# Moving a decay chain under a linear layer, and a compression under memory attention, in a two-block transformer kernel

## What is computed

```python
# gated linear attention (GLA) layer; memory of 256 tokens, 4 heads of 128
q, k, v, r, alr, mq = split_cols(h @ w_in, [256, 256, 512, 512, 16, 512])
log_a = log_sigmoid(alr @ w_alpha + b_alpha) / 16
o = gla_chunked(q, k, v, log_a)          # cumulative decays scale q and k; state scan over chunks
o = rmsnorm(o, g_head) * silu(r)
m = mem_attend(mq, mem_k, mem_v)         # softmax(mq mem_k^T) mem_v
x = x + concat([o, m]) @ w_out

# sparse attention (NSA) layer
k_c, v_c, k_s, v_s, k_w, v_w = split6(rmsnorm(x) @ w_kv)
k_cmp = gelu(blocks(k_c + pe_k) @ w_ck1) @ w_ck2      # 31 compressed blocks; the same for v
p_cmp = masked_softmax(q k_cmp^T + bias) * gate       # "compressed weights"
o = p_cmp v_cmp + gate * attention(q, k_s, v_s) + gate * attention(q, k_w, v_w)
m = mem_attend(mq, mem_k, mem_v)
x = x + concat([o, m]) @ w_out
```

## Time and profile before

| | us |
|---|---|
| median of 3 runs | 3510.04 (3506.98 to 3519.47) |
| the profiled execution | 3506.27 (its span 3504.5) |
| PE busy in it | 3334.3 (95%) |
| DVE busy | 1746.9 (50%) |
| ACT busy | 1274.3 (36%) |
| POOL busy | 334.0 (10%) |

### The profile page before, as it was taken

The page is one execution under the profiler, slowest core; times in us unless marked ns, Lnnn a source line. Parts: engine busy times, 40 slices in busy tenths (PEclk is TensorE's granted clock), DMA queues, the critical chain, the costliest instruction groups (busy, mean ns, idle before and its releaser), DMA issues. The chain is left out here.

```text
span 3504.5 us, 52430 instructions
## 1 busy us (share of the span) xinstructions
PE 3334.3 (95%) x21106; PEld 2738.0 (78%) x21106; DVE 1746.9 (50%) x2634; ACT 1274.3 (36%) x1870; POOL 334.0 (10%) x277
## 2 busy tenths in 40 slices
PE   7999999799999999999899999978999997899998
PEld 5888879588888888879778888866888875578886
DVE  4444364554443444365454443446665355666642
ACT  3222355632222222355642222334222232542222
POOL 0000315300000000133500000010000001400000
PEclk9999999899999999999999999999999998999999
DMA  3332320023332333320023333302333250023332
GB/s 115 96 100 99 107 72 4 29 90 97 97 103 90 98 96 103 112 78 15 15 79 96 97 103 102 126 29 74 99 97 104 95 176 10 13 79 97 98 102 81
DMA packets 73605, 295.72 MB, mean 84 GB/s; under 512 B 8160, under 2 KB 9056, under 8 KB 72288
## 3 DMA queue, kind: packets, MB, share of 16 engines
q1 hardware_dynamic: 73440, 293.32, 25.9%
HBM read 291.19 MB, written 2.10 MB: 84 GB/s over the span
## 5 line engine op out<-in xcount | busy, mean ns | idle before, releaser
L438 PE MATMUL bank<-src_hi,tile_hi 128*128 128x512 f32 x2736 | 1078.6, 394 | 26.2 <-DVE tile_lo L514 25.3
L440 PE MATMUL bank<-src_hi,tile_lo 128*128 128x512 f32 x2736 | 1065.5, 389 | 0.0
L439 PE MATMUL bank<-src_lo,tile_hi 128*128 128x512 f32 x2736 | 1065.1, 389 | 0.0
L514 DVE TENSOR_TENSOR tile_lo<-raw_tiles,tile_hi 128x1024 fp32r<-128x1024 f32 (+1 forms) x486 | 625.2, 1312 | 76.1 <-ACT tile_hi L465 59.4
L438 PEld LDWEIGHTS bank<-src_hi,tile_hi 128*128 128x128 f32 x2736 | 514.1, 188 | 145.3 <-DVE tile_lo L514 25.7
L439 PEld LDWEIGHTS bank<-src_lo,tile_hi 128*128 128x128 f32 x2736 | 514.3, 188 | 112.3 <-issue 6.7
L440 PEld LDWEIGHTS bank<-src_hi,tile_lo 128*128 128x128 f32 x2736 | 514.0, 188 | 107.4
L465 ACT ACTIVATE tile_hi<-raw_tiles 128x1024 fp32r<-128x1024 f32 (+1 forms) x486 | 526.9, 1112 | 103.4 <-DMA raw_tiles<-in_b_in 33.1
L438 PE MATMUL bank<-hid_hi,tile_hi 128*128 128x512 f32 x1312 | 514.3, 392 | 25.2 <-DVE tile_lo L514 25.2
L439 PE MATMUL bank<-hid_lo,tile_hi 128*128 128x512 f32 x1312 | 513.4, 391 | 0.0
L440 PE MATMUL bank<-hid_hi,tile_lo 128*128 128x512 f32 x1312 | 513.3, 391 | 0.0
(11 more groups left out here) (329 smaller groups left out, 3177.6 us busy)
## 6 DMA issues: line engine op xcount, KB each, us to landing
raw_tiles<-in_gu SPq DMA_DIRECT2D x264, 512.0 KB, 3.5
raw_tiles<-in_down SPq DMA_DIRECT2D x96, 704.0 KB, 4.0
raw_tiles<-in_w_in SPq DMA_DIRECT2D x46, 512.0 KB, 3.5
raw_tiles<-in_a_in SPq DMA_DIRECT2D x17, 512.0 KB, 3.6
raw_tiles<-in_w_out SPq DMA_DIRECT2D x16, 512.0 KB, 3.6
raw_tiles<-in_w_mem SPq DMA_DIRECT2D x16, 512.0 KB, 3.5
masks<-in_masks SPq DMA_DIRECT2D x4, 1948.0 KB, 8.6
raw_tiles<-in_b_in SPq DMA_DIRECT2D x9, 512.0 KB, 3.5
```

Source lines behind the costliest of these rows:

```text
L438: nc.tensor.matmul(bank, wh, hi[:, kk, 0:p.n], start=(kk == 0), stop=False)
L439: nc.tensor.matmul(bank, wh, lo[:, kk, 0:p.n], start=False, stop=False)
L440: mm = nc.tensor.matmul(bank, wl, hi[:, kk, 0:p.n], start=False, stop=last and (p.kind == "gated" or s == p.h - 1))
L514: v.tensor_tensor(self.tile_lo[:, t, 0:kc * P], self.tile_raw[:, t, 0:kc * P], self.tile_hi[:, t, 0:kc * P].bitcast(F32), ALU.subtract).th ...
```

## The change

1. **Decay chain under `a_in`.** The 17 tiles are taken in a new order: `alr` first, then q, k, r, v, mq. The decay chain (and the four SiLU) leaves the GLA phase and hangs on the tiles of `a_in`, in the steps given by `DECAYED_AT = (7, 12)`, its temporaries now in `mix`. PE's code for `a_in` is no longer a loop but written out.
2. **GLA steps closer.** The scaled k is turned in step 0, v in step 1, key-value products in steps 3 and 6 (before 9 and 11), scans in 3, 4, 6, 7 (before 9 to 12), scores in 9, outputs in 12 and 13, squares in 14 and 15. The prefetch of the output weights no longer waits for the decays.
3. **NSA.** Gates, compression and compressed weights are no phases of their own: they are hung on the steps of the memory attention, which moves ahead of `attention_pairs`. The prefetch for the output product is issued in `attention_pairs`.
4. 56 semaphores for each of two alternating phases instead of 48.

```diff
+A_IN_ORDER = [16, *range(0, 4), *range(8, 12), *range(4, 8), *range(12, 16)]
+DECAYED_AT = (7, 12)
@@ chain, tensor
-                    if p.heads:
+                    if p.heads or p.decays:
                         for i in range(1, p.m):
                             tile(i, i, 0)
+                                self.decay_products(pe, own, p, i)
@@ chain, scalar and vector: at the end of body(i)
+                        if p.decays:
+                            self.decay_activations(act, own, p, i)
+                            self.decay_vectors(dve, own, p, i)
@@
+    def decay_products(self, pe, own, p, i):
+        if i == DECAYED_AT[0] - 1:
+            pe.wait_ge(own["beside_loaded"], p.beside_landed)
+            pe.wait_ge(own["bank_free"], p.tiles + 1)
+            for cc in range(2):
+                self.nc.tensor.matmul(self.banks[2 + cc][:, :], w[0:16, cc * P:(cc + 1) * P], self.pj(16)[0:16, :], ...)
+    def decay_activations(self, act, own, p, i):
+        for cc, first in enumerate(DECAYED_AT):
+            if i == first + 1:
+                act.wait_ge(own["magnitude"], cc + 1)
+                nc.scalar.activation(mag, mag, ACT.Exp, scale=-1.0)
+                nc.scalar.activation(mag, mag, ACT.Ln, bias=self.c("one"))
+            if i == first + 3:
+                act.wait_ge(own["summed_up"], cc + 1)
+                nc.scalar.activation(ein, cum, ACT.Exp, scale=1.0 / 16)
+                nc.scalar.activation(eout, cum, ACT.Exp, scale=-1.0 / 16)
+        if i == DECAYED_AT[1] + 2:
+            for h in range(4):
+                nc.scalar.activation(self.pj(8 + h), self.pj(8 + h), ACT.Silu)
+    def decay_vectors(self, dve, own, p, i):
+            if i == first:        # bias, absolute value, minimum: 3 operations
+            if i == first + 2:    # waits logged_z; subtraction, scan
+            if i == first + 4:    # waits decays_ready; k*eout, q*ein, ends, kt
@@ gla_products
+        if s == 0:    # turn the scaled k: 8 transposes
+        if s == 1:    # waits kt_copied_a, kt_copied_v, values_copied; turn v: 16 transposes
-        if s in (9, 11):
+        if s in (3, 6):   # key-value products; s == 6 waits scanned 16
-        if s == 7:
+        if s == 9:        # scores; waits scanned 30
-        if s in (13, 14):
+        if s in (12, 13): # outputs; waits masked
@@ memory_attention(nsa=True)
+    def nsa_sums(self, pe, own, s):
+        if s == 0:        # 4 transposes of the gates
+        if 2 <= s <= 5:   # compression: 8 of 32 matmuls in each step, waits arranged
+        if s in (7, 9):   # waits gelu_ready; 2 transposes
+        if s == 10:       # waits gelu_copied; 8 matmuls
+        if s == 12:       # waits kept; 16 score matmuls with the compressed keys
+        if s in (16, 17): # waits weights_ready; 8 transposes each
+    def nsa_activations(self, act, own, s):
+        # s == 0: Sigmoid; s in (4, 6): Tanh; s in (13, 14): Exp; s in (16, 18): two copies each
+    def nsa_vectors(self, dve, own, s):
+        # s < 4: two arrange operations each; (4, 6): five GELU operations; (5, 7): the sixth; (7, 9): a copy
+        # 8: eight bias operations; 10: four copies; (12, 13): add, max, floor, subtract; (14, 15): sum, reciprocal, gates, multiply
@@ nsa_layer
-        self.nsa_gates(gates_flat)
-        self.compress(...)
-        self.compressed_weights(k_cmp, gates, turned)
-        self.attention_pairs(pairs, HD ** -0.5, values=[(kv[:, 3, :], vs), (kv[:, 5, :], vw)])
-        self.memory_attention(4, [self.mix[:, 4 + c, :] for c in range(4)], ahead=("b_out", 0, KD, 2))
+        self.memory_attention(4, [self.mix[:, 4 + c, :] for c in range(4)], nsa=True)
+        self.attention_pairs(pairs, HD ** -0.5, values=[(kv[:, 3, :], vs), (kv[:, 5, :], vw)], ahead=("b_out", 0, KD, 2))
```

More of the change, by code:

```diff
@@ L1623, in gla_weights @@
         return self.pj(17)[:, 0:2 * P]
[L1625 to L1631, removed]
+    GLA_SIGNALS = ("v_turned", "v_copied_a", "v_copied_v", "scores", "masked", "kt_turned", "kt_copied_a", "kt_copied_v", "kv_product", "scanned",
+                   "product", "stored", "squared", "summed", "logged", "rstd_ready", "normed")
@@ L1654, in gla_products @@
         if s == 0:
[L1655 to L1665, removed]
-                    mm = nc.tensor.transpose(tile(banks[6 + h % 2], i), tile(self.pj(4 + h), i), self.c("ident", P))
-                mm.then_inc(own["v_turned"], 1)
@@ L1668, in gla_products @@
-        if s == 7:
-            pe.wait_ge(own["scaled"], 2)
-            pe.wait_ge(own["v_copied_a"], 2)
-            pe.wait_ge(own["v_copied_v"], 2)
             for cc in range(2):
                 for i in range(NT):
-                    for e in range(2):
-                        mm = nc.tensor.matmul(tile(banks[4 + 2 * cc + e], i), tile(self.pj(2 + cc)[rows[e], :], i), tile(self.pj(cc)[rows[e], :], i),
-                                              start=True, stop=True)
-                mm.then_inc(own["scores"], 1)
@@ L1698, in gla_products @@
             mm.then_inc(own["kv_product"], 1)
-        if s in (13, 14):
-            cc = s - 13
-            if cc == 0:
-                pe.wait_ge(own["scanned"], 2 * (NGC - 1))
+        if s == 9:
+            pe.wait_ge(own["scanned"], 2 * (NGC - 1))
+            for cc in range(2):
+                for i in range(NT):
+                    for e in range(2):
+                        mm = nc.tensor.matmul(tile(banks[4 + 2 * cc + e], i), tile(self.pj(2 + cc)[rows[e], :], i), tile(self.pj(cc)[rows[e], :], i),
+                                              start=True, stop=True)
+                mm.then_inc(own["scores"], 1)
+        if s in (12, 13):
+            cc = s - 12
+            pe.wait_ge(own["masked"], 2 * cc + 2)
             for e in range(2):
@@ L1805, in gla_vectors @@
+        if s in (3, 4, 6, 7):
+            first = 4 * (s - 3 - s // 5)
+            for c in range(first, min(first + 4, NGC - 1)):
                 dve.wait_ge(own["kv_product"], 1 + c // 8)
@@ new lines, in weights_memory, with nsa_cleared @@
+    def weights_memory(self):
+        both = [self.units("arena", at, 2).rearrange("p u t -> p (u t)").rearrange("p (c i e w) -> p c i e w", c=4, i=NT, e=2) for at in (28, 30)]
+        return both + [self.small[:, i * 32:i * 32 + 32].rearrange("p (c i e) -> p c i e", c=4, i=NT) for i in range(3)]
+    def nsa_cleared(self, pool, own):
+        for out in self.compressed():
+            self.nc.gpsimd.memset(out, 0.0).then_inc(own["cleared"], 1)
+        self.nc.gpsimd.memset(self.units("arena", 28, 2), NEG).then_inc(own["cleared"], 1)
@@ L2094, in build @@
         core.first_mixers(1)
[L2095 removed]
+        a_in = projected(("a_in", 0, KD), 17, "x", core.proj[:, :, 1:T + 1], order=A_IN_ORDER, decays=True, beside=[core.masks_load(), (core.gla_weights(), dram["w_alpha"])])
         core.chain([*core.layer_end(1, p2("g_mix", 0)), a_in, core.memory_products(0)], source="mix", prefetched=2)
```

500 lines of the change are left out of this document (246 added, 254 removed).

## The result

The changed kernel takes **3476.93 us** (median of 4 runs, 3476.23 to 3479.74) against 3510.56 of the kernel before (the median of 4 runs by now, 3506.98 to 3519.47); the ratio of the two is 0.990, with a 95% interval of 0.9888 to 0.9913. The forecast was 3476. Why the two differences differ is told with experiment 1.

A forecast was written before the change was run, and what follows sets the result against it. PE, busy for 95% of the span, was taken as the bound, so shorter PE waits pay. Profiled 3506.3 − 25.8 (GLA) + 1.8 (`a_in`) − 7.9 (NSA) = 3474.4, plus 1.6 for the median: 3476 us, range 3463 to 3491.

The forecast's parts named there:

- Parts 1 and 2: Decay chain under `a_in` costs 1.8 us; GLA phase falls to 63 us, a gain of 25.8.
- part 3: NSA layer: compression and scores hung on memory attention steps, 64.8 us, a gain of 7.9.
- the walk: Step-by-step sum of each engine's new order with earlier durations: GLA 61.0 us, NSA 63.3 us, before allowances.
- The 1.6 set on top: Whole kernel: added to the profiled execution's 3474.4 us to forecast the median, 3476.
- all at half clock: GLA outputs: two pairs take 11.9 us at that rate, 6 at the full clock, taken 8.5.
- The allowance of 2: GLA phase: 2 us added to the 61.0 for tightly counted hand-overs and uncounted clock losses.
- R5: GLA phase: the decays don't leave its path, only 5 us go, 3500 us; chance 0.03.
- R1: NSA phase gives nothing back: POOL multiplies slowed beside DVE, lower clock, 3482 us; chance 0.13.
- The rule of the Trainium skill cited in the prediction: NSA phase: two-input DVE operations exclude POOL's 16 multiplies, an estimate of 11 us, time 3485.
- R2: GLA phase stays slow because PE is cold and late: 73 instead of 63, 3485 us; chance 0.10.
- R3: GLA and NSA phases both stay behind: 3492 us; chance 0.06.
- R4: `a_in`, tiles 8 to 17: two ACT waits break the ring of splits, +54, 3529 us; chance 0.03.

The follow-up runs named there:

- experiment 1: Each half of the change alone against the kernel before: `g_only` 3487.76 us, `n_only` 3505.25 us, kernel before 3512.72 us.
- `g_only`: Decay chain under `a_in` and new GLA steps, NSA layer as in the kernel before: 3487.76 us against 3512.72, ratio 0.9929.
- `n_only`: New NSA layer, `a_in` and GLA phase as in the kernel before: 3505.25 us against 3512.72, ratio 0.9975.
- `after`: First profile of the changed kernel, unaltered: span 3478.0 us; median of its 4 runs 3476.93 us.
- `after_again`: The changed kernel, unaltered, run once more on the third chip: 3477.03 us (4 runs).
- `weights_on_act`: The changed kernel with the softmax multiply of both memory phases on ACT instead of POOL: 3479.50 us.
- Experiment 6: Five variants of the changed kernel; second source's blocks arranged in step 1: 3475.43 us; that plus 22 unused transposes ahead of the gates wait: 3470.65 us.
- experiment 4: The changed kernel with four useless 512-column DVE operations in each of bodies 8 to 15 of `a_in`: 3483.86 us (1 run).
- experiment 2: The changed kernel with the GLA phase's own work on its earlier steps, decays still under `a_in`: 3489.77 us, ratio to before 0.9936.
- experiment 5: The changed kernel with each of the two decay products in `a_in` issued three times: 3488.68 us (1 run).
- experiment 3: The changed kernel with each pair's GLA output products issued twice: 3494.70 us (1 run).

## Why the prediction was right, and where it was off

**The total.** Parts 1 and 2 together were to bring 24.0 and brought 25.0 (`g_only`); part 3 was to bring 7.9 and brought 7.5 (`n_only`). Both halves are right on their own, not only their sum, within intervals of about 6 and 3 to either side. Part of this is luck, and the profiled executions show it. For them the forecast was 3474.4, and the one of the changed kernel took 3479.74. Set against the trace of before, as the walk did it, `a_in` cost 0.3 more than forecast, the GLA phase was 2.5 too long, the NSA memory phase 3.4, and the attention between pairs, forecast as unchanged, 1.3. The walk was too short in each of these, and the trace of before is one in which the old phases were short (experiment 1); in the medians the two errors nearly cancel. The 1.6 set on top for the median had the wrong sign: for the changed kernel the median lay 2.8 below the profiled execution, not above it.

**`a_in`: 1.8 forecast, 2.1 measured.** The mis-sized term is the product: taken as 0.90 from the spacing in `w_in`, it has a row of 0.99; the other 0.16 lies at the change from the weight tiles' products to these and back, which no run tests alone. DVE and ACT cost nothing, and the split that the last operations delay is taken from the wait of the earlier trace rows, all as forecast.

**The GLA phase: 63 forecast, 65.5 and 65.3 in the two traces, 63.4 in `g_only`.** By segments, forecast then measured: start to first key-value product 8.7 and 8.7; to the end of the scans 14.9 and 14.9; scores and masks 7.6 and 8.7; outputs 14.9 and 18.6; sums to the end 14.9 and 14.3 (trace `after`). The step that failed is the reading of the earlier trace rows as "all at half clock": the outputs of before were at 1.00 and 0.90, so there was almost nothing to win back. A pair takes 5.5 at the full clock against the 4.25 taken, and with some lower clock in the second pair the two are 2.9 of the segment's missing 3.7. The scores were taken at 2.5. They ran at the lower clock before (3.79, granted 0.50), and in this trace they do again, 3.54 at a granted 0.55. But in `after_again`, `g_only` and `weights_on_act`, with the same steps, they took 2.06; in `after_again` the key-value product ahead of them was slow instead (1.67, here 1.21), and its phase took 65.3 all the same. So where the clock is lowered changes from one execution to the next, and one trace can't say what the place of the scores costs. The allowance of 2 for such things covered about half of it.

**The NSA phase: 64.8 forecast, 68.3 and 66.9.** Here the walk is 2 to 3.5 short, and the terms of it are found. The third quarter of the compression was taken without a lower clock of its own and with a short wait; it waits 2.54 and runs at 5.35. The reason is DVE's order: the second source's blocks stand behind a row maximum whose score stands on PE behind the first quarter, so DVE idles for 7 us and then both engines wait for each other in turn. Experiment 6 took that away and the phase was 63.4. Of the 2.6 that the cold start costs (6.29 against 3.66), 1.9 were foreseen (8.96 against 7.07 for a half). The steps 6 to 11 took 2.6 each instead of 2.3, 1.8 in all, at the lower clock of 0.61 in part. That the gain still came to 7.5 is probably because the layer of before is worth more than the trace of before showed: 170.0 there, 175.2 in the other. There was no table load ahead of the phase's two tanh: only the pair around the sigmoid. The Trainium skill, "ScalarE: Activation LUTs", "Table sets: the hidden batching unit", has tanh in the set of exp, and the trace agrees.

**The rivals.** By the prediction's own sum the rivals' prices leave out the 1.6 that the forecast adds, and R5 comes to 3495, not 3500. R1: refuted by `n_only` (5 to 12 less), and the 20 of its premise by `weights_on_act`. The port conflict exists as a price of single operations. POOL's multiplies in the NSA phase, beside DVE's arranging (two inputs in SBUF) and elsewhere:

```profile
2893.60 1.66 POOL L1538 TENSOR_SCALAR arena<-arena,small 128x256 f32<-128x256 f32 x1 [3.52 <-DVE small L1619]
...
2907.74 0.92 POOL L1538 TENSOR_SCALAR arena<-arena,small 128x256 f32<-128x256 f32 x1 [2.89 <-DVE small L1619]
```

Four of 16 were slowed (the next one took 1.55, a pair beside the bias operations took 3.17), 2.7 in all. Each of the first two began while an arranging operation was running; the one at 2907.74 began 0.5 ahead of such an operation and took its usual 0.92. The 1.30 of the earlier trace rows, too, began inside the subtraction ahead of the scan (2313.35 to 2314.04, both inputs in SBUF), not inside the scan. The rule of the Trainium skill cited in the prediction, by which all 16 could wait for 11 us, agrees with the trace in kind and not in the sum: the estimate let every multiply meet such an operation. R2 and R3 (73 in the GLA phase) didn't come: the ten traces with the new phase unaltered or with the multiply moved have 63.4 to 69.3. R4 is refuted by the spacing of 5.44 in the changed kernel (with experiment 4 as far as it reaches), R5 by experiment 2.

**Left open:** why the same instructions are granted different clocks from one execution to the next (old GLA phase 89.1 and 97.9, attention between pairs 94.5 to 102.6 over all fourteen traces). It decides several us in every comparison of single profiles.

## What to carry to other kernels

DVE and ACT work moved from a hand-over-bound phase into a PE-bound one was free here as long as each body's total stayed under its tile time, and where it didn't, it cost about the excess, up to the 1.2 us that was tried; what moves on PE itself is paid in full. Before a slow row is put down to the lower clock, ask for the granted clock of that very stretch. Where two in-order engines feed each other, look for independent work that stands behind a wait (here the second source's blocks): moving it ahead, and keeping PE busy in the idle just before a long product, took 6.4 of 3477 off (four runs each). When two profiles differ by a few us, compare the medians first.

## What the hardware showed

- PE's clock fell from 1.00 to 0.50 with PE busy for 100% of the time, in a run of twelve records of 16-row products (experiment 5), and again to 0.56 behind gap-free output products (experiment 3). The first was seen in one trace. The Trainium skill, "TensorE: Matmul & The Clock Gate", "Why this matters for your kernels", names idle gaps of PE as what to avoid; here there was none, so by that rule alone the clock wouldn't have fallen and experiment 5 would have shown 4.0 instead of 6.7.
- A record of 32 columns takes 59 ns at the full clock (3.54 for 60) and 110 ns at the lower one (6.61 for 60); one of 128 columns 122 ns (1.95 for 16) and 213 to 230 ns at 0.53 to 0.56 (3.40 and 3.68 for 16).
- Unused transposes ahead of the first quarter brought it to 3.67 and 3.64 instead of 6.29, both times. What they cost themselves differed: 22 of them directly behind other work took 2.56, 28 behind an idle of 2.45 ran at a granted 0.65, took 4.95 and ate the gain.
